# Down projections of a decoder trunk: three of eleven weight units as seven block products in place of eight

## The reference, cut to what matters

```
h = h + 0.5 * swiglu(rms_norm(h, ln), w_gate, w_up, w_down)

def swiglu(x, w_gate, w_up, w_down):
    return (jax.nn.silu(x @ w_gate) * (x @ w_up)) @ w_down
```

## Time and profile before

| | |
|---|---|
| time, median of 3 runs | 919.54 us (918.83 to 919.99) |
| profiled execution | 919.42 us, span 917.6 us |
| PE busy | 905.8 us, 99% of the span |
| DVE, ACT, POOL busy | 63%, 51%, 10% |
| granted TensorE clock | 0.998 of full |
| chain that ended last | PE 91%, DVE 4%, DMA 2% |
| DMA | 202.86 MB, mean 221 GB/s |

### The profile page before, as it was taken

The page is one execution under the profiler, slowest core; times in us unless marked ns, Lnnn a source line. Parts: engine busy times, 40 slices in busy tenths (PEclk is TensorE's granted clock), DMA queues, the critical chain, the costliest instruction groups (busy, mean ns, idle before and its releaser), DMA issues.

```text
span 917.6 us, 11621 instructions
## 1 busy us (share of the span) xinstructions
PE 905.8 (99%) x4195; PEld 745.5 (81%) x4195; DVE 574.0 (63%) x724; ACT 471.6 (51%) x635; POOL 90.7 (10%) x170
## 2 busy tenths in 40 slices
PE   8999999999999999999999999999999999999997
PEld 7888888888888888888888888888876788888885
DVE  5656663574787766665467566644588776656542
ACT  6554443565685654444346445433478664444431
POOL 1100005623311100000002000000030000000000
PEclk9999999999999999999999999999999999999999
DMA  9898778558733888876557888874563388887611
GB/s 306 258 296 240 240 243 243 209 180 289 234 98 93 263 266 261 246 261 230 178 162 231 251 249 249 301 243 171 196 230 110 121 279 272 263 252 285 228 71 46
DMA packets 169758, 202.86 MB, mean 221 GB/s; under 512 B 15160, under 2 KB 139136, under 8 KB 169712
## 3 DMA queue, kind: packets, MB, share of 16 engines
q1 hardware_dynamic: 168752, 201.37, 67.5%
q0 software_dynamic: 512, 0.36, 0.4%
q10 hardware_dynamic: 448, 0.53, 0.2%
HBM read 184.39 MB, written 17.83 MB: 220 GB/s over the span
## 4 chain that ended last, share of the span: by engine, by line
PE 91%; DVE 4%; DMA 2%; issue 1%; ACT 1%; SPq 1%; POOL 0%; POOLq 0%; DVEq 0%; ACTq 0%
PE bank L535 58%; PE bank L574 18%; PE bank L580 9%; PE bank L596 2%; PE bank L764 1%; PE bank L639 1%; DVE w_lo L1767 1%; PE bank L795 1%; DMA raw<-in_ffn_w_up 1%; DMA x_bounce<-silu 0%; PE bank L817 0%; PE bank L741 0%; SPq L1055 0%; ACT junk L1399 0%; DVE hT_lo L1767 0%
## 5 line engine op out<-in xcount | busy, mean ns | idle before, releaser
L1767 DVE TENSOR_TENSOR w_lo<-raw,w_hi 128x2048 fp32r<-128x2048 f32 x149 | 340.2, 2292 | 185.5 <-ACT w_hi L1380 185.1
L1380 ACT ACTIVATE w_hi<-raw 128x2048 fp32r<-128x2048 f32 x154 | 294.4, 1916 | 194.3 <-PE bank L580 97.6
L535 PE MATMUL bank<-w_hi,xT_hi 128*128 128x512 f32 x816 | 318.8, 391 | 0.2 <-DVE w_lo L1774 0.2
L535 PE MATMUL bank<-w_lo,xT_hi 128*128 128x512 f32 x816 | 317.6, 389 | 0.0
L535 PE MATMUL bank<-w_hi,xT_lo 128*128 128x512 f32 x816 | 307.9, 389 | 0.0
L535 PEld LDWEIGHTS bank<-w_hi,xT_hi 128*128 128x128 f32 x816 | 153.2, 188 | 33.1 <-DVE w_lo L1774 0.6
L535 PEld LDWEIGHTS bank<-w_hi,xT_lo 128*128 128x128 f32 x816 | 153.2, 188 | 31.9
L535 PEld LDWEIGHTS bank<-w_lo,xT_hi 128*128 128x128 f32 x816 | 153.2, 188 | 31.3
L574 PE MATMUL bank<-w_hi,hT_hi 128*128 128x512 f32 x348 | 135.6, 390 | 0.0
L574 PE MATMUL bank<-w_lo,hT_hi 128*128 128x512 f32 x348 | 135.4, 389 | 0.0
L580 PE MATMUL bank<-w_hi,hT_lo 128*128 128x512 f32 x348 | 107.1, 389 | 0.0
(11 more groups left out here) (182 smaller groups left out, 599.7 us busy)
## 6 DMA issues: line engine op xcount, KB each, us to landing
raw<-in_ffn_w_down SPq DMA_DIRECT2D x88, 512.0 KB, 5.1
raw<-in_ffn_w_gate SPq DMA_DIRECT2D x86, 512.0 KB, 5.9
raw<-in_ffn_w_up SPq DMA_DIRECT2D x86, 512.0 KB, 7.0
raw<-in_a_w_qkv SPq DMA_DIRECT2D x24, 512.0 KB, 5.6
h_bounce<-silu SPq DMA_DIRECT2D x40, 256.0 KB, 7.0
xn<-h_bounce SPq DMA_DIRECT2D x160, 64.0 KB, 3.0
xn<-x_bounce SPq DMA_DIRECT2D x64, 64.0 KB, 2.0
raw<-in_a_w_o SPq DMA_DIRECT2D x8, 512.0 KB, 5.3
```

Source lines behind the costliest of these rows:

```text
L535: mm = nc.tensor.matmul(bank[b][:, :], xs[:, kt, own(pos)], ws[:, slot(u), cols], start=(kt == 0 and i == 0), stop=(kt == KT - 1 and i == 2))
L1380: nc.scalar.activation(w_parts(u)[0], raw[:, slot(u), :], ACT.Copy).then_inc(s_hi, 1)
L1767: nc.vector.tensor_tensor(lo, raw[:, slot(u), :], hi.bitcast(F32), ALU.subtract).then_inc(s_lo, 1)
```

## The change

A unit of w_down is a 2x2 block matrix B (two hidden tiles k by two halves j), and what it meets is a 2x2 block matrix A of activations (two pos by the two tiles). In three of the eleven units the eight block products are replaced by seven (Winograd's form), each again three matmuls: 21 for 24. The sums of activations (S1 to S4) are made in the loop turns, when the tiles land; the sums of weights (t1, T2, T4, T3) when the unit has landed. The block t1 is written over its raw block before the unit is split; T2, T4, T3 stand in `t_raw`, which has the place of xT_lo, and are then split into t_hi (the place of xT_hi) and t_lo. In the first feed-forward DVE forms the sums of weights, in the other three GpSimd. Four of the seven products gather in banks 4 to 7; `seven_added` puts them into x. The order in which units of w_down are taken changes (DN_ORDER), each of the first seven is used for both pos at once, the copy `h_hi`/`h_lo` of pos 1 moves ahead of the split of unit 4g+5, and the bias and norm vectors, whose buffer the sums of activations share, are loaded later.

```diff
+DN_ORDER = [1, 3, 0, 5, 2, 6, 4, 7, 8, 9, 10]
+SEVEN = [2, 4, 6]
 # tensor block
+            def seven(f, u, n):
...
+                pe.wait_ge(s_h_sums_lo, seven_no(f, n))
+                pe.wait_ge(s_t_lo, seven_no(f, n))
+                for b in (4, 5, 6, 7) if begin else ():
+                    take(b)
+                three(6, s_tile(3), t_tile(T3), begin, end)
+                three(5, s_tile(2), t_tile(T2), begin, end)
+                three(acc(1, 0), a_tile(1, 1), t_tile(T4)).then_inc(s_t_used, 1)
+                unit_ready(u)
+                three(7, s_tile(1), b_tile(0, 1), begin, end)
+                three(4, a_tile(0, 0), b_tile(0, 0), begin, end)
+                three(acc(0, 0), a_tile(0, 1), b_tile(1, 0))
+                three(acc(0, 1), s_tile(4), b_tile(1, 1)).then_inc(s_used, 1)
...
-                down((0, 1, 2), 0)
+                down((0,), 0)
                 pe.wait_ge(s_hT_lo[1], block_no(f, H_BLOCKS - 2))
-                down((0, 1, 2), 1)
-                down((3, 4, 5, 6), 0)
-                down((3, 4, 5, 6), 1)
+                down((0,), 1)
+                for i in range(1, SEVEN_END):
+                    if i in SEVEN:
+                        seven(f, u0 + GU_UNITS + i, SEVEN.index(i))
+                    else:
+                        down((i,), 0)
+                        down((i,), 1)
 # sync block, loads of w_down and of the vectors
+                        if i - UNITS_HELD in SEVEN:
+                            sp.wait_ge(s_t_sums, seven_no(f, SEVEN.index(i - UNITS_HELD)))
...
-                down(*range(8, DN_UNITS))
+                down(8, 9)
+                if "b_b_q" in vectors:
+                    vector("b_b_q", u0)
+                down(10)
...
 # gpsimd block, called as t_sums(1, ..), t_sums(2, ..), t_sums(3, ..)
+            def t_sums(f, u0):
+                for n, i in enumerate(SEVEN):
+                    u = u0 + GU_UNITS + i
+                    pool.wait_ge(s_raw[slot(u)], 32 * (u // UNITS_HELD + 1))
+                    nc.gpsimd.tensor_tensor(raw_tile(u, 0, 1), raw_tile(u, 0, 1), raw_tile(u, 0, 0),
+                                            ALU.add).then_inc(s_t1, 1)
+                    if n == 0:
+                        pool.wait_ge(s_used, u0 + GU_UNITS)
+                    else:
+                        pool.wait_ge(s_t_used, seven_no(f, n) - 1)
+                    pool.wait_ge(s_t1, seven_no(f, n))
+                    t2, t4, t3 = [t_raw[:, BANK * j:BANK * (j + 1)] for j in range(3)]
+                    link(nc.gpsimd.tensor_tensor(t2, raw_tile(u, 0, 1), raw_tile(u, 1, 1), ALU.add))
+                    nc.gpsimd.tensor_tensor(t4, t2, raw_tile(u, 1, 0), ALU.add)
+                    nc.gpsimd.tensor_tensor(t3, t2, raw_tile(u, 0, 0), ALU.subtract).then_inc(s_t_sums, 1)
 # scalar block, turn_of
                     split(u0 + 4 * g + 4, turn)
-                    split(u0 + 4 * g + 5, turn)
                     if g:
                         h_hi(1, g - 1, 0 if turn is None else turn)
+                    split(u0 + 4 * g + 5, turn)
...
                     silu_gate(1, 0, g, turn)
+                    if turn is not None:
+                        h_sums_high(f, turn)
 # scalar block, down projection
-                split(u0 + 24)
+                split_with_t1(u0 + 24, f, 0)
                 split(u0 + 25)
                 silu_gate(1, 0, 5)
-                split(u0 + 26)
+                t_high(f, 0)
+                split_with_t1(u0 + 26, f, 1)
                 h_hi(1, 4)
-                for i in range(27, 30):
-                    split(u0 + i)
+                split(u0 + 27)
+                t_high(f, 1)
+                split_with_t1(u0 + 28, f, 2)
+                split(u0 + 29)
                 h_last_hi(0)
                 h_last_hi(1)
+                t_high(f, 2)
                 for i in range(30, 33):
                     split(u0 + i)
+                act.wait_ge(s_used, u0 + GU_UNITS + SEVEN_END)
+                nc.scalar.activation(p1_copy, bank[4][:, :], ACT.Copy).then_inc(s_read[4], 1)
 # vector block, turn_of
                     split(u0 + 4 * g + 4, turn)
-                    split(u0 + 4 * g + 5, turn)
                     if g:
                         h_lo(1, g - 1, 0 if turn is None else turn)
+                    if turn is not None:
+                        h_sum(f, turn)
+                    split(u0 + 4 * g + 5, turn)
...
                     mul(1, 0)
+                    if turn is not None:
+                        h_sum_low(f, turn)
 # vector block, down projection
+                if f == 0:
+                    t_first(f, u0 + 24, 0)
                 split(u0 + 24)
                 split(u0 + 25)
                 h_last_turned(0)
...
                 mul(1, 0, 5)
                 h_last_turned(1)
+                if f == 0:
+                    t_sums(f, u0 + 24, 0)
+                    t_first(f, u0 + 26, 1)
+                t_low(f, 0)
                 split(u0 + 26)
                 h_lo(1, 4)
-                for i in range(27, 30):
-                    split(u0 + i)
+                split(u0 + 27)
+                if f == 0:
+                    t_sums(f, u0 + 26, 1)
+                    t_first(f, u0 + 28, 2)
+                t_low(f, 1)
+                split(u0 + 28)
+                split(u0 + 29)
                 h_last_lo(0)
                 h_last_lo(1)
+                if f == 0:
+                    t_sums(f, u0 + 28, 2)
+                t_low(f, 2)
                 for i in range(30, 33):
                     split(u0 + i)
+                seven_added(f)
```

More of the change, by code:

```diff
@@ L139, in trunk @@
         xT_hi = sb("xT_hi", [P, KT, SEQ], F32R)
+        with nc.sbuf_tensor("t_raw", [P, KT * SEQ], F32) as t_raw:
+            pass
         xT_lo = sb("xT_lo", [P, KT, SEQ], F32R)
@@ L558, in last_rows_pass, with rows_pass @@
                 mm.then_inc(s_used, 1)
-            def rows_pass(u, kt0, n_kt, pos, lhs_hi, lhs_lo, key, part=None, lo_ready=None):
+            def rows_pass(u, kt0, n_kt, pos, lhs_hi, lhs_lo, key, part=None, lo_ready=None, first=None):
+                if first is None:
+                    first = kt0 == 0 and part != 1
                 if pos == 0 and (u, part) == (U_WO_A + 3, 0):
@@ L565, in rows_pass @@
                     unit_ready(u)
-                if kt0 == 0 and part != 1:
+                if first:
                     take(acc(pos, 0))
@@ L574, in rows_pass @@
                             nc.tensor.matmul(bank[acc(pos, j)][:, :], lhs_hi[:, kt, own(pos)],
-                                             ws[:, slot(u), cols], start=(kt == 0 and i == 0), stop=False)
+                                             ws[:, slot(u), cols], start=(first and kt == kt0 and i == 0),
+                                             stop=False)
                     if k == 0 and lo_ready:
@@ L590, in rows_pass, with three, a_tile, s_tile @@
                         note((*key, pos, j), acc(pos, j))
+            def three(b, lhs, rhs, start=False, stop=False):
+                (l_hi, l_lo), (r_hi, r_lo) = lhs, rhs
+                nc.tensor.matmul(bank[b][:, :], l_hi, r_hi, start=start, stop=False)
+                nc.tensor.matmul(bank[b][:, :], l_hi, r_lo, start=False, stop=False)
+                return nc.tensor.matmul(bank[b][:, :], l_lo, r_hi, start=False, stop=stop)
+            def seven(f, u, n):
+                def a_tile(pos, k):
+                    kt = 2 * DN_ORDER[SEVEN[n]] + k
+                    return hT_hi[:, kt, own(pos)], hT_lo[:, kt, own(pos)]
+                def s_tile(i):
+                    return h_sums[:, n, 0, P * (i - 1):P * i], h_sums[:, n, 1, P * (i - 1):P * i]
+                def b_tile(k, j):
+                    cols = slice(D * k + BANK * j, D * k + BANK * (j + 1))
+                    return w_hi[:, slot(u), cols], w_lo[:, slot(u), cols]
+                def t_tile(i):
+                    cols = slice(BANK * i, BANK * (i + 1))
+                    return t_hi[:, cols], t_lo[:, cols]
+                T2, T4, T3 = range(3)
+                begin, end = n == 0, n == N_SEVEN - 1
+                pe.wait_ge(s_h_sums_lo, seven_no(f, n))
[10 more added lines that the diff above has]
+                three(acc(0, 1), s_tile(4), b_tile(1, 1)).then_inc(s_used, 1)
+                for b in (4, 5, 6, 7) if end else ():
+                    note(("seven", f, b), b)
             def transposes(srcs, b, key, turn=None):
@@ L1380, in split, with split_with_t1, t_high, h_sums_high @@
                 nc.scalar.activation(w_parts(u)[0], raw[:, slot(u), :], ACT.Copy).then_inc(s_hi, 1)
+            def split_with_t1(u, f, n):
+                act.wait_ge(s_t1, seven_no(f, n))
+                split(u)
+            def t_high(f, n):
+                act.wait_ge(s_t_sums, seven_no(f, n))
+                nc.scalar.activation(t_hi[:, 0:3 * BANK], t_raw[:, 0:3 * BANK], ACT.Copy).then_inc(s_t_hi, 1)
+            def h_sums_high(f, turn):
```

(17 more changed lines are left out.)

92 lines of the change are left out of this document (80 added, 12 removed).

## The result

The kernel after takes 945.75 us (median of 4 runs, 944.18 to 948.48), the one before, on the same chip, 919.66. The ratio is 1.0288, with a 95% interval from 1.0262 to 1.0314: slower by 26.1 us. The forecast was slower by 5.6, and 945.75 lies outside the range given. The profiled execution took 946.41, span 944.6.

The account below looks back on a forecast made before the run. TensorE was taken as the bound, busy 905.8 of 917.6 us. Removed matmuls -8.2, sevens in the last three feed-forwards +9.9, the first +1.4 and gate-up loop +2.5 gave +5.6: 919.42 to 925.0 us, range 914 to 933.

Parts of the forecast that it names:

- The order of the units costs nothing: Down projection: the new unit order adds no time; it releases a weight slot after 5.44 instead of 10.9 us.
- Removed matmuls: Three units in four feed-forwards need 21 matmuls for 24: 36 x 0.2267 = 8.2 us saved, all on the path.
- GpSimd's add at 1.2: Sums of weights: a 128x512 GpSimd add takes 1.2 us, between bounds of 0.46 and 1.84.
- The lock: GpSimd adds and DVE splits wait for each other's whole instruction: add ends 1.1 us after split, split 2.15 after add.
- Sevens 1 and 2: Second and third seven-product units, last three feed-forwards: PE waits 1.7 and 1.5 us for the weight sums' low part.
- First feed-forward: Down projection where DVE adds: PE waits 0.4, 0.4 and 0.6 us at the three seven-product units, 1.4 in all.
- Loop: Gate-up turn 1: late splits cost 0.85 us in the second feed-forward, 1.6 in the fourth; 2.5 together.
- the exchange did not fall behind: Rival, gate-up loop: a longer exchange cycle costs about 1 us in ten more turns, 935; chance 0.11 shared with dear adds.
- SP's waits: Down projection: SP waiting for the sums delays loads of units 6, 8 and 10, but 8 us cover a landing.
- `seven_added`: End of the down projection: eight 512-column operations, 5.5 us, hidden by 1 us; otherwise at most 1 to 2 us once.
- a spacing above 0.259: Rival, seven-product units: matmul spacing above 0.259 us would cancel the gain; no row shows it, no separate chance given.
- Sums hidden: Rival: lock absent or adds nearer 0.46 us, so sums are ready for sevens 1 and 2; 912.9 to 915.4, chance 0.21.

Follow-up runs that it names:

- x2: Kernel before, with only TensorE's order of units in the down projection changed to the new one, eight products everywhere, no sums: 934.91 us, ratio 1.0166.
- x4: Kernel after, with pos 1's copy and subtraction, the activation sums and their splits moved back behind the splits of units 4g+5 and 4g+6: 940.99 us.
- z1c: Kernel before, with one block product left out in units 2, 4 and 6 of each down projection, output incomplete: 910.92 us, ratio 0.9909.
- x1: Kernel after, with the last silu and `mul` of pos 1 moved ahead of split(25): 931.22 us, ratio to the kernel before 1.013.
- y1c: x1 plus, in the last three feed-forwards, DVE making the sums' low parts ahead of weight splits not yet due: 921.32 us, ratio to before 1.0018.
- y3c: y1c and x4 together, GpSimd still adding the weight sums in the last three feed-forwards: 912.30 us, ratio to the kernel before 0.9929.
- x3: Kernel after, with DVE forming the sums of weights in all four feed-forwards and none on GpSimd: 939.77 us, ratio to the kernel before 1.022.

## Why the prediction was wrong

**The step that failed** is "The order of the units costs nothing". It looked at what the order releases (slots of weights) and not at what it takes. The wait of PE for bank 2 stood in the code, `take` at the first matmul of pos 1, and so did the position of `mul` behind split(25) in DVE's list. Both ends could be read from the trace of before: DVE's second split ends at T + 4.5 (419.36 + 2.29 in the earlier trace rows), the short operations with `mul` among them follow, and pos 1 now comes at T + 2.7. That alone gives 2.6 a time, or 10.4, which is what x2 measured. The prediction even counted those short operations, for seven 0, but as load on DVE, not as what PE was waiting for. The longer split under the adds brings 1.8 more (12.2 in x4), the later start of the splits behind the moved copy and sums another 2.6, which makes 14.8; and on top comes the clock with 5.1, of which at least 3.4 stand right behind these waits.

**Point by point.**
- Removed matmuls, -8.2: right (z1c, 8.2). Count 4159: right.
- GpSimd's add at 1.2: measured 1.30. t_high 1.48 and t_low 1.77: 1.49 and 1.76.
- The lock: right in both forms. The add of 423.74 met the split that ended at 425.30 and ended at 426.45, 1.15 behind it (predicted 1.1). The split of 425.71 ended 2.14 after that add (predicted 2.15).
- Sevens 1 and 2, 1.7 and 1.5 in each of three feed-forwards: 1.54 and 1.56 in the kernel after, 1.67 and 1.53 in x1, where the bank's wait doesn't shift the schedule. First feed-forward, 1.4: 0.37, since only one of its three sevens waits; the schedule was a little late there. In all 9.7 against 11.3.
- Loop, 2.5: 4.3, and a half-clock stretch of 1.7 behind one wait. The fourth feed-forward came as predicted, 1.25 + 0.42 against 1.0 + 0.6. In the second, PE ran out at 346.1, which is 19.04 into the turn, so the turn began at 327.1 and the copy at S + 16.2, against S + 14.2 before: the block landed 2 us later, and PE waited 2.18 against 0.85 predicted. Why the block landed later wasn't resolved. The first lost 0.42 against none. That later turns lose nothing: right, so the exchange did not fall behind.
- SP's waits, `seven_added`, the moved vectors and a spacing above 0.259: no row of PE's waits points to any of them. Right.
- The clock: no term at all. The earlier trace rows and a span with no wait above 1.6 us gave no sight of it, but once a wait was forecast, that question was open.

The terms that were in the sum came to 9.7 + 4.3 - 8.2 = +5.8 against +5.6. That it is so close is luck: the sevens cost 1.6 less than predicted and the loop 1.8 more. What was left out came to 14.8 + 5.1, and 1.3 of rest; the whole is 27.0 of span (944.6 - 917.6). "Sums hidden" was wrong as a forecast for this kernel, but y1c and y3c have the sevens' sums ready in time by taking the splits out of the chain, and y3c, which has only 0.5 of the bank's waits and none of the loop's, takes 912.3, just under the 912.9 to 915.4 of that rival.

## What to carry to other kernels

When the order of matmuls changes, list for each first use not only the operands but the PSUM bank that it writes, find the instruction that frees it, and count what stands ahead of that instruction on its engine. On an engine at 99%, an edit that "only reorders" is worth a run of its own: here it cost nearly twice what the algebra saved. GpSimd is a free helper only while VectorE runs nothing that locks it out; in the last three feed-forwards PE waited 9.3 us for its adds among the splits and not at all between them (y1c, y3c), at the price of moving lines.

## What the runs showed of the hardware

TensorE's granted clock fell from 2.4 to 1.2 GHz for 3.41 us at a time, around or right behind waits of 2.2 to 5.1 us in the middle of otherwise unbroken work, at a cost of 1.7 each: three times in the kernel after, three in x2, four in x3. In x4 two stretches were 6.83 long and began before PE resumed. It isn't certain: in the kernel after, waits of 2.9 and 3.2 had no such stretch, and in x2 three of four equal waits of 2.6 had one. In x4 a wait of 2.6 had none either, and in x3 one of 2.8 had one. What decides was not settled. The records of the kernels whose work has no wait of 2.2 us or more show it nowhere but at the very end; the longest such wait, 1.7 in x1 and y1c, has none.

GpSimd and VectorE hold each other up for whole instructions. A 128x512 GpSimd add takes 1.29 alone, and 2.7 to 3.4 when a 128x2048 split of VectorE lies across it; that split takes 2.29 alone and 2.9 to 3.4 across an add.
